# Down stage of a hybrid S5 / mLSTM / PEER block: pieces of the gates asked for in other steps, slots of the last block spread otherwise

## The reference, cut to what matters

```python
    def block(args):
        tb, eb, gb = args
        u = jnp.take(expert_u, eb, axis=0)
        act = jax.nn.gelu(jnp.einsum('ted,td->te', u, tb)) * gb
        vv = jnp.take(expert_v, eb, axis=0)
        return jnp.einsum('te,ted->td', act, vv)
```

## Time and profile before

| | us |
|---|---|
| median of 3 runs | 3960.4 (3959.0 to 3963.62) |
| profiled execution, its time | 3964.08 |
| its span | 3962.5 |
| PE busy | 3813.3 (96%) |
| DVE busy | 2704.9 (68%) |
| POOL busy | 1406.9 (36%) |
| ACT busy | 1219.4 (31%) |
| down stage, first L407 to last | 2946.1 to 3909.6 |

### The profile page before, as it was taken

The page is one execution under the profiler, slowest core; times in us unless marked ns, Lnnn a source line. Parts: engine busy times, 40 slices in busy tenths (PEclk is TensorE's granted clock), DMA queues, the critical chain, the costliest instruction groups (busy, mean ns, idle before and its releaser), DMA issues.

```text
span 3962.5 us, 53089 instructions
## 1 busy us (share of the span) xinstructions
PE 3813.3 (96%) x19109; PEld 3268.4 (82%) x19109; DVE 2704.9 (68%) x3547; ACT 1219.4 (31%) x1299; POOL 1406.9 (36%) x921
## 2 busy tenths in 40 slices
PE   8999999999999999999999999999999889899997
PEld 5888777787788788888888887777889889899997
DVE  7565888559532755454767665777885777788895
ACT  4333222344322322222333332222223333322222
POOL 1100000332211344545000055888553434456653
PEclk9999999999999999999999999999999999999999
DMA  4565555665753555455777777777877999888994
GB/s 171 191 220 166 164 168 168 221 218 174 245 204 117 183 172 185 165 186 190 232 250 256 255 249 245 263 265 249 304 266 270 342 337 351 318 337 337 350 352 169
DMA packets 272219, 941.22 MB, mean 238 GB/s; under 512 B 37793, under 2 KB 83889, under 8 KB 194633
## 3 DMA queue, kind: packets, MB, share of 16 engines
q1 hardware_dynamic: 94448, 446.73, 31.2%
q0 software_dynamic: 71504, 283.37, 20.7%
q10 hardware_dynamic: 106176, 210.00, 16.8%
HBM read 893.10 MB, written 238.31 MB: 286 GB/s over the span
## 4 chain that ended last, share of the span: by engine, by line
PE 49%; DVE 11%; DMA 7%; POOL 4%; issue 4%; ACT 3%; SPq 0%; ACTq 0%; DVEq 0%; POOLq 0%
PE mm L2134 13%; PE mm L2135 12%; PE mm L2136 12%; DMA raw<-stream 5%; DVE wlo L1239 4%; DVE acc L2034 3%; POOL gv L705 2%; POOL el L698 2%; PE pv L2134 2%; PE pv L2136 2%; PE pv L2135 2%; ACT whi L788 2%; DMA gl<-up_d 1%; PE sc L2134 1%; PE sc L2135 1%
## 5 line engine op out<-in xcount | busy, mean ns | idle before, releaser
L1239 DVE TENSOR_TENSOR wlo<-raw,whi 128x2048 fp32r<-128x2048 f32 x329 | 755.9, 2298 | 480.0 <-ACT whi L788 440.3
L788 ACT ACTIVATE whi<-raw 128x2048 fp32r<-128x2048 f32 x378 | 723.5, 1914 | 449.6 <-issue 194.5
L2134 PE MATMUL mm<-t_hi,whi 128*128 128x512 f32 x2048 | 804.2, 393 | 34.8 <-DVE wlo L1239 28.9
L2135 PE MATMUL mm<-t_lo,whi 128*128 128x512 f32 x2048 | 800.4, 391 | 0.0
L2136 PE MATMUL mm<-t_hi,wlo 128*128 128x512 f32 x2048 | 799.6, 390 | 0.0
L2034 DVE SCALAR_TENSOR_TENSOR acc<-gv,ac,acc 128x2048 f32<-128x2048 f32 x254 | 596.3, 2348 | 80.1 <-DMA gv<-ev_d,idx_v 66.6
L2134 PEld LDWEIGHTS mm<-t_hi,whi 128*128 128x128 f32 x2048 | 386.4, 189 | 124.2 <-issue 26.0
L2136 PEld LDWEIGHTS mm<-t_hi,wlo 128*128 128x128 f32 x2048 | 386.3, 189 | 81.3
L2135 PEld LDWEIGHTS mm<-t_lo,whi 128*128 128x128 f32 x2048 | 386.5, 189 | 77.6
L744 POOL DMA_INDIRECT gv<-ev_d,idx_v x128 | 244.5, 1910 | 432.6 <-DVE acc L2034 359.8
L2134 PE MATMUL mm<-hn_hi,whi 128*128 128x512 f32 x960 | 377.6, 393 | 8.2 <-DVE wlo L1239 8.2
(11 more groups left out here) (476 smaller groups left out, 7346.1 us busy)
## 6 DMA issues: line engine op xcount, KB each, us to landing
raw<-stream SPq DMA_DIRECT2D x380, 1024.0 KB
ev_d<-stream ACTq DMA_DIRECT2D x128, 1024.0 KB
up_d<-sgl ACTq DMA_DIRECT2D x128, 256.0 KB
g_d<-gst ACTq DMA_DIRECT2D x12, 2048.0 KB
spill<-stage ACTq DMA_DIRECT2D x44, 256.0 KB, 2.0
gg<-g_d SPq DMA_DIRECT2D x28, 384.0 KB
gl<-up_d SPq DMA_DIRECT2D x56, 192.0 KB
gl<-up_d SPq DMA_DIRECT2D x72, 128.0 KB
```

The lines of the kernel that those rows point to most:

```text
L788: act.activation(whi[:, k, :], raw[:, k, :], ACT.Copy).then_inc(hi_done, 1)
L1239: dve.tensor_tensor(wlo[:, k, :], raw[:, k, :], whi[:, k, :].bitcast(F32), ALU.subtract)\
L2134: pe.matmul(out, lh, rh, start=start, stop=False)
L2135: pe.matmul(out, lh, rl, start=False, stop=False)
```

## The change

`SLOTS2` gives each group from 1 on its number of slots. Before: 7 in groups 1 to 8, 11 in groups 9 to 12, 12 in 13 and 14, 4 in 15. After: 6 in groups 1 to 4, 7 in 5 to 8, 12 in 9 to 14, 4 in 15. The four pieces of the gates are asked for in steps 2, 4, 6 and 7 instead of 1, 3, 5 and 7, and all of them wait for one and the same thing, the group's first gate product. `lead`, by how many slots the loads of `el` are ahead at the start, is written otherwise: the first two batches together, 14 before, 12 after.

```diff
-SLOTS2 = _counts(SLOTS, (7, G1 - 1), (11, 4), (12, 2), (4, 1))
+SLOTS2 = _counts(SLOTS, (6, 4), (7, 4), (12, 6), (4, 1))
+GATE_STEPS = (2, 4, 6, 7)
...
-                    if v % 2 == 1 and g + 2 < GROUPS_D:
-
-                        sp.wait_ge(gated_done, 8 * g + 8 + v)
+                    if v in GATE_STEPS and g + 2 < GROUPS_D:
+
+                        sp.wait_ge(gated_done, 8 * g + 9)
                         nb = (BLOCKS if g + 2 >= G1 else TE // 32) // 4
-                        ns = slice(nb * (v // 2), nb * (v // 2) + nb)
+                        piece = GATE_STEPS.index(v)
+                        ns = slice(nb * piece, nb * piece + nb)
                         sp.dma_start(gg[:, g % 2, ns, :], gg_src[g + 2][:, ns, :]).then_inc(gn_in, 16)
...
-            lead = SLOTS2[1][0] + SLOTS2[1][1]
+            lead = 2 * SLOTS2[1][1]
             for s in range(lead):
                 activation(s)
             for s in range(3, SLOTS):
                 rows(s)
                 activation(s - 3 + lead)
```

## The result

The changed kernel takes 3975.93 us (median of 8 runs, 3967.47 to 3983.48), the kernel before 3960.74 (8 runs, 3957.93 to 3965.11): a ratio of 1.0032, with a 95% interval from 1.0021 to 1.0043. It is 15 us slower. The profiled execution of the changed kernel is the quickest of its eight, 3967.47 us with a span of 3965.9, so that the two traces differ by only 3.4 us. What follows on the trace therefore explains where time moved; how much the change costs is told by the medians.

What follows compares the result with a forecast made beforehand. Transfers bound the narrow half; in the wide half TensorE was always busy and VectorE without slack at 12 slots. -28 and +46 gave +18 us on the profiled run (3982.1), a median of about 3978; range 3948 to 3996.

Steps and rivals of the forecast that it cites:

- the two terms: Down stage: narrow half (groups 1 to 8) -28 us, wide half (groups 9 to 14) +46 us.
- Part 4: Wide half: lead falls to 12, el lands late, L2049 waits 8 us; +41.5 over groups 10 to 14, +4.5 group 9.
- el lands fast: Rival, wide half: el overtakes the gather, waits about 4 us, wide half +23, total -5, 3955 us; chance 0.13.
- el isn't late: Rival, wide half: L2049 does not wait for el, total -26, 3934 us; chance 0.09.
- part 1: Narrow half: reordered SyncE queue brings every second raw up to 2.5 us earlier; with four gathers saved, -28 us.
- Part 3: Groups 9 to 12: one slot more raises VectorE's work to 66.9 us a group, together +2 us.
- Part 2: Groups 1 to 4: one slot less takes out four 1 MB gathers, 12 to 12.5 us.
- only its bytes: Rival, narrow half: reorder gives nothing, only the gathers' 12 us are gained; total +34, 3994 us; chance 0.15.

Runs made afterwards that it cites:

- gl first: Kernel before with gl of the odd step issued ahead of the gate-product wait and gg, raw still behind all of it: 3935.44 us, ratio 0.9933.

## Why the prediction was right, and where a term was off

**The forecast holds.** 3978 forecast, 3975.93 measured; slower, inside its own range of 3966 to 3990. But the two terms were both too small (in the trace -46.8 for -28, +53.5 for +46), and the gain of the narrow half lies outside the 20 to 36 that the forecast named. In the trace the parts give +3.5 us where I had +18. That the median came within 2 us of the forecast is in part luck: the two errors have opposite signs, and the median lies 8.5 us above the traced execution. The profiled execution came out at 3967.5 where I had 3982; that the other runs of the same kernel are up to 16 us longer, when those of before spread over 7, no view that I have explains, and it stays open.

**Part 4, el.** Right in mechanism, place and number: six waits, 7.73, 8.30, 9.41, 8.79, 8.74 and 8.75 us for my 8, with leads of 12, 13 and 14 giving 8.6, 3.7 and 0 us on average. In group 9 I had chosen 5 and it was 7.73. That its wait is shorter than the others holds in every run with late el (6.02 against 9.2 to 9.6 with the new slots alone, none against 3.3 to 4.0 with a lead of 13); that the single slot in the last step of the group before is the reason was not tried. The waits cost 8.7 us a group on average, (455.08 - 402.92) / 6, where I had 8. The granted clock fell to 0.95 over the wide half as foreseen (1.00 without the waits).

**The rival "el lands fast", and the page.** It is refuted. The Trainium skill, in "DMA: Bandwidth & Descriptors", section "Anatomy of one DMA — SWDGE (gpsimd) path", puts a request at about 2.0 us and its bytes at 436 GB/s, which is an estimated 4.4 us for the gather of 1 MB. This case does not agree: the el behind such a gather was there 9.7 and 10.0 us after the gather's issue, and the DMA engines were 0.84 busy from group 11 to 12. That the full queues are the reason, as the prediction says, is argued; no run here has a gather in empty ones.

**The rival "el isn't late"** is refuted by the same six waits. It shows what was at stake: with the lead put right the change gives 0.9908, near its 3934 but better, by the gain of part 1.

**Part 3, the 12th slot.** I said +2 us. The wide half without waits for el takes 402.9 us with 12-slot groups (lead 14) and 400.8 with the old slots and the new order: +2.2.

**Part 2, four gathers.** I said 12; the slots alone save 13.2 us of the narrow half, at the same 335 GB/s.

**Part 1, the mis-sized term.** "The gate products' own waits for gl should vanish too; they mostly overlap the raw waits and I count them at nothing" is the step that failed. The order alone is worth 34.6 us in the trace (406.58 for 441.18) and 36 in the medians, not some 16, and gl first, with raw nearly as late as ever, gives 25 of them. VectorE's 19.9 us of waiting for gl stand in its order of work ahead of the next split, which TensorE waits for; that they, and not another effect of asking for gl early, make the 25 us is argued from the two traces. The rate that I took from groups 10 to 12, 348 GB/s, was too low: 364 over the half and 373 in a group of 7 slots. The upper end of my own bound (44 us at group 13's 362 GB/s) was the right one. I also misread the chain: its longest loads of raw took 12.84 and 12.18 us, not 11.5, and the one of 11.52 us asked for at 3405.36 did not go out behind gg. And what part 1 calls a new order is, in the requests that follow one another, the old one without the hold: the piece stands behind one raw and ahead of a gl in both kernels.

**The rival "only its bytes"** (rate unchanged) is refuted by the order alone: same bytes, 363 GB/s.

**What would beat both.** The new order with el 14 or more slots ahead: 3922.79 and 3919.75 us, 0.9908 and 0.9897. The slots add nothing that can be measured to the order alone (3923.83); their gain of 8 to 12 us in the narrow half (398.5, 396.1 and 394.4 us against 406.6) can be seen only in the traces.

## What to carry to other kernels

A number that is derived from the table that one changes (here the lead, from the batch sizes) changes with it: work out for the last item of a batch when its load can be issued and when it is read, for every batch size. In a queue that issues in order, put the small request that the next product needs ahead of the big one, and keep no wait in front of either that is there only for a third: here that wait was most of the loss, and it went away with a looser condition or one step later in the program alike. Where many engines wait on each other in turn, a wait counted as "covered by another" should be tried with only that one removed.

## What the runs showed of the hardware

With the same bytes in one queue, asking for a 128 KB load ahead of a wait and a 256 KB load gave 25 us, and asking for a 1 MB load ahead of all of these cost 146 us. The issue of an indirect load, gv or el, kept GpSimd busy for 0.94 to 3.00 us, so that the last of four in a row went out 6.8 us behind the first (3571.18 and 3577.95 in the kernel after). The el, 512 bytes (128 values of 4 bytes), took 6.4 to 8.75 us from its issue when it stood behind a gather of 1 MB. The DMA engines moved 364 GB/s over 394 us and 373 over 51, at a busy share of 0.94 and 0.96, where the kernel before had 335 at 0.90.
